# A beginning in another order, head norms with two buffers, and convolution and gate products in steps inside the attentions

## The reference, cut to what matters

```python
# first block, l = 0, 1; D = 1024
mod = silu(c) @ w_ada[l] + b_ada[l]            # 6 x 1024: shift, scale, gate for mixer and experts
h = rmsnorm(x, g_mix[l]) * (1 + sc1) + sh1
p = h @ w_in[l]        # keys, values, 8 + 8 query heads of 64, convolution 3 x 512, gates 3 x 1024
q = rope(rmsnorm(q, qg)); k = rope(rmsnorm(k, kg))       # norm over each head's 64
o_a = global attention; o_b = window attention with sinks
u = c_gate * x_in
o_c = b_gate * sum(w[j] * shifted(u, j) for j in range(3))
merged = sum over branches: sigmoid(gate) * (o @ w_branch)
x = x + gt1 * (merged @ w_out); then experts
# second block
h = rmsnorm(x, gain); p = h @ w_in
o = concat(banded(q_a, k_a, v_a) * silu(g_a), dilated(q_b, k_b, v_b) * silu(g_b))
x = x + o @ w_out
```

## Time and profile before

| | |
|---|---|
| median of 3 runs | 3480.6 us (3479.89 to 3485.04) |
| profiled execution | 3479.74 us, span 3477.7 us, mean granted TensorE clock 0.979 |
| PE busy | 3198.9 us, 92% |
| DVE, ACT busy | 1075.6 us (31%), 641.6 us (18%) |
| DMA | 551.85 MB, mean 159 GB/s |

### The profile page before, as it was taken

The page is one execution under the profiler, slowest core; times in us unless marked ns, Lnnn a source line. Parts: engine busy times, 40 slices in busy tenths (PEclk is TensorE's granted clock), DMA queues, the critical chain, the costliest instruction groups (busy, mean ns, idle before and its releaser), DMA issues. The chain is left out here.

```text
span 3477.7 us, 35357 instructions
## 1 busy us (share of the span) xinstructions
PE 3198.9 (92%) x13776; PEld 1568.4 (45%) x13776; DVE 1075.6 (31%) x1541; ACT 641.6 (18%) x1124; POOL 16.7 (0%) x35
## 2 busy tenths in 40 slices
PE   6989999999997999999988999999789889888978
PEld 3565555555553333333343654444423324343544
DVE  2566644555422010101036561011300010036241
ACT  3137500000011111111121560000111101021151
POOL 1000000000000000000000000000000000000000
PEclk8999999999998999999999999999899999999999
DMA  7020033443414878787830201223198988942200
GB/s 222 0 73 1 1 121 115 145 150 105 139 49 154 304 285 307 285 304 289 303 93 0 73 1 55 73 73 103 37 376 346 404 355 352 405 114 49 61 1 25
DMA packets 305434, 551.85 MB, mean 159 GB/s; under 512 B 62744, under 2 KB 145960, under 8 KB 305160
## 3 DMA queue, kind: packets, MB, share of 16 engines
q1 hardware_dynamic: 303376, 546.53, 44.2%
q0 software_dynamic: 1600, 3.20, 0.3%
q10 hardware_dynamic: 312, 0.05, 0.0%
HBM read 547.63 MB, written 2.10 MB: 158 GB/s over the span
## 5 line engine op out<-in xcount | busy, mean ns | idle before, releaser
L736 PE MATMUL ps<-hT,ring 128*128 128x512 f32 (+1 forms) x2576 | 969.6, 534 | 29.5 <-ACT hT L1259 27.7
L736 PEld LDWEIGHTS ps<-hT,ring 128*128 128x128 f32 x2576 | 492.6, 192 | 494.1 <-issue 464.4
L1013 PE MATMUL ps<-ring,hT 128*64 128x512 f32 x1536 | 356.9, 600 | 64.4 <-DMA ring<-in_w_e_up 35.5
L992 PE MATMUL ps<-ring,hT 128*64 128x512 f32 x1536 | 350.8, 598 | 1.5 <-ACT hT L1259 1.5
L1013 PEld LDWEIGHTS ps<-ring,hT 128*64 128x64 f32 x1536 | 100.2, 136 | 311.1 <-issue 159.3
L1906 DVE SCALAR_TENSOR_TENSOR xT<-ps,mod,xT 128x512 f32<-128x512 f32 x96 | 63.5, 662 | 498.7 <-PE ps L1099 281.1
L992 PEld LDWEIGHTS ps<-ring,hT 128*64 128x64 f32 x1536 | 101.8, 136 | 235.6 <-issue 235.1
L736 PE MATMUL ps<-obuf,ring 128*128 128x512 f32 (+1 forms) x512 | 198.5, 540 | 1.3 <-issue 1.3
L998 PE MATMUL ps<-ring,hT 128*32 128x512 f32 x1536 | 184.7, 598 | 0.0
L1591 DVE SCALAR_TENSOR_TENSOR vbuf<-ring,silc,vbuf 128x1024 f32<-128x1024 f32 x140 | 179.9, 1285 | 5.7
L1259 ACT ACTIVATE prob<-ps 128x512 f32<-128x512 f32 (+1 forms) x56 | 38.6, 688 | 673.7 <-PE ps L736 673.7
(11 more groups left out here) (223 smaller groups left out, 2471.0 us busy)
## 6 DMA issues: line engine op xcount, KB each, us to landing
ring<-in_w_e_gate SPq DMA_DIRECT2D x128, 512.0 KB, 7.2
ring<-in_w_e_up SPq DMA_DIRECT2D x128, 512.0 KB, 7.1
ring<-in_w_e_down SPq DMA_DIRECT2D x128, 512.0 KB, 6.9
ring<-in_w_e_gate SPq DMA_DIRECT2D x64, 1024.0 KB, 10.6
ring<-in_w_e_up SPq DMA_DIRECT2D x64, 1024.0 KB, 10.7
ring<-in_w_e_down SPq DMA_DIRECT2D x64, 1024.0 KB, 10.7
ring<-in_w_in SPq DMA_DIRECT2D x49, 1024.0 KB, 5.6
ring<-in_w_ada SPq DMA_DIRECT2D x48, 1024.0 KB, 6.8
```

What stands on the lines that cost most here:

```text
L736: mm = pe.matmul(ps[:, b + a:b + e], lhs[:, k, :], rhs[:, k, a:e], start=k == 0, stop=k == nk - 1)
L992: mm = pe.matmul(ps[e * CX:(e + 1) * CX, b + pair * 512:b + (pair + 1) * 512], lhs[:, k, s0:s0 + CX], expert_dst(0, slot, e)[:, k % 2, :], ...
L1013: mm = pe.matmul(ps[e * CX:(e + 1) * CX, b + h * 512:b + (h + 1) * 512], lhs[:, k, s0:s0 + CX], expert_dst(1, slot, 0)[:, e, h * 512:(h + ...
```

## The change

- **Beginning.** c and c_ctx are ACT's first loads and are turned on their own (`cond`), so silu(c) doesn't wait for the parameters. SP issues ten chunk loads before the larger part of the constants. The two first modulation groups are split along the input features instead of the output (`adf`, four chunks for each group, contiguous rows), added up in one PSUM bank and turned once for each group (`adft`). ACT squares each tile of x as soon as it is copied, DVE adds the squares, and PE sums once (`ns`). The meeting is gone.
- **Norms.** The reciprocal and the scaling are done for 512 columns first, then for the rest; the gain moves from DVE's scaling to ACT's shift (as its scale); the first product waits only for the half that it reads.
- **Head norms.** Squares alternate between `sq` and a row of `prob`, roots between `rs` and another; the sine product goes to a third row; rotations come one tile later.
- **Steps in attentions.** `conv_c` and `conv_x` of layers 0 and 1, and the last four `silg`, are taken out of the dense list. They are cut into steps (two matmuls of 512 columns, or four of 256), one behind the scores of each unit, in PSUM bank `BANK[4]`, which gets a slot of its own (`SIDE`). All value sums share `BANK[3]`. In layer 2 the transposed exponentials of the banded half stand in the unused columns of `hT`.
- **Silu.** x * sigmoid(x) becomes x * (1 + tanh(x/2)), and the factor 0.5 goes into the copy of the inverted row sums. The gates of layers 0 and 1 keep the sigmoid.

`with_modulation` is not changed.

```diff
+        roots = [rs, pr[:, 1, :]]
+        squares = [sq, pr[:, 2, :]]
+        turn_term = pr[:, 0, 0:NX]
...
+        def side_steps(l):
+            steps = []
+            if l == 2:
+                for d in range(4, 8):
+                    steps += [[("side", l, "silg", d, 0, q)] for q in range(4)]
+                    steps[-1].append(("silg", l, d))
+                return steps
+            for m in range(4):
+                for w in ("conv_c", "conv_x"):
+                    for a in range(2 - l):
+                        steps += [[("side", l, w, m, a, q)] for q in range((4, 2)[a])]
+                        steps[-1].append((w, l, m, a))
+            return steps
...
                 if s < n:
                     order.append(("S", l, s))
+                if side:
+                    order += side.pop(0)
...
-                if rots:
+                if len(rots) > 1:
                     order.append(rots.pop(0))
...
-            conv = [(f"conv_{w}", l, m) for hf in range(2) for w in "cxb" for m in (2 * hf, 2 * hf + 1)]
+            conv = [("conv_b", l, m) for m in range(4)]
...
-            first += [("v", 2, 1), ("v", 2, 2)] + [("silg", 2, d) for d in range(8)]
+            first += [("v", 2, 1), ("v", 2, 2)] + [("silg", 2, d) for d in range(4)]
...
-        FIRST = [(w, 0, n + (w == "ada")) for n in range(-1, 8) for w in ("ada", "adat") if 0 <= n + (w == "ada") < 8]
+        FIRST = [("adf", 0, 1, q) for q in range(4)] + [("ns", 0), ("adft", 0, 1)]
+        FIRST += [("adf", 0, 0, q) for q in range(4)] + [("adft", 0, 0), ("pv", 1)]
...
+                if kind == "side":
+                    w, m, a, q = j[2:]
+                    key = (w, l, m) + ((a,) if l < 2 else ())
+                    cn, slot = weights(chunk_of(j)[0])
...
+                    lo, hi, per = (0, 512, 2) if a == 0 else (512, NT, 4)
+                    for k in range(per * q, per * (q + 1)):
+                        mm = pe.matmul(ps[:, BANK[SIDE]:BANK[SIDE] + hi - lo], ring3(slot)[:, k, m % 2 * P:(m % 2 + 1) * P],
+                                       h3[:, k, lo:hi], start=k == 0, stop=k == KD - 1)
...
+                elif kind == "ns":
+                    pe.wait_ge(first_added, 1)
+                    b = begin(("norm", 0, "mix"))
+                    for a, e in halves(NT):
+                        mm = pe.matmul(ps[:, b + a:b + e], ones[:, :], h3[:, 0, a:e], start=True, stop=True)
+                    part(mm, ("norm", 0, "mix"))
...
-                        if h % 2 == 0 and n >= 2:
-                            pe.wait_ge(oT_ready.sem, n - 1)
-                    b = BANK[3 + n % 2] + h % 2 * 2 * P
+                        if h % 2 == 0 and n:
+                            pe.wait_ge(oT_ready.sem, n)
+                    b = BANK[HEAD_SUMS] + h % 2 * 2 * P
...
             sp.dma_start(tok[:, 4:6, :], ctx_in[0].rearrange("(t p) d -> p t d", p=P)).then_inc(s_x, 16)
+            for n in range(RING + 4):
+                load(n)
             sp.dma_start(con[:, C_ROT:C_HELD], consts[:, C_ROT:C_HELD]).then_inc(s_const, 16)
...
+            for d in range(KD):
+                if d % 2:
+                    A.need(xT_ready, d)
+                else:
+                    b = A.read(("xT", d))
+                    A.do(sc.copy(xT[:, d, :], ps[:, b:b + NT]))
+                    A.release(("xT", d))
+                A.do(func(h3[:, d, :], xT[:, d, :], ACT.Square), sq_ready, ("n", 0, "mix", d))
...
             def norm(ph, w):
-                key = ("norm",) + ph
-                V.need(rms_ready, key)
-                V.do(v.reciprocal(rs[:, 0:w], rs[:, 0:w]))
...
+                V.need(rms_ready, ("norm",) + ph)
+                for a, e in halves(w):
+                    V.do(v.reciprocal(rs[:, a:e], rs[:, a:e]))
+                    scaled(ph, a, e, 0, KD)
...
-                    V.do(v.tensor_tensor(sg2[:, d, :], g, ps[:, b:b + w], ALU.mult), gate_used, j)
+                    V.do(v.scalar_tensor_tensor(sg2[:, d, :], g, 1.0, ps[:, b:b + w], ALU.add, ALU.mult), gate_used, j)
```

More of the change, by code:

```diff
@@ L289, in attention_order @@
                     order.append(("T", l, s - 1, 2))
+            assert not side
             return order
@@ L720, in norm_sum @@
                 for d in range(KD):
-                    need(sq_ready, ("n",) + ph + (d,))
-                    for a, e in halves(w):
-                        mm = pe.matmul(ps[:, b + a:b + e], ones[:, :], m3[:, d, a:e], start=d == 0, stop=d == KD - 1)
-                part(mm, key)
+                    norm_piece(b, ph, m3, d, w)
+                part(norm_piece.last, key)
             seen_h = set()
@@ L1115, in _ @@
                 part(mm, ("xT", d))
-            for l in range(DEPTH):
-                pe.wait_ge(s_param[l], PARAM_DMAS[l] * 16)
-                b = begin(("pv", l))
-                rows = PROWS[l]
-                part(pe.transpose(ps[:, b:b + rows], prob[0:rows, l, 0:P], ident[0:rows, 0:rows]), ("pv", l))
-            meet()
+            run(("pv", 0))
             for j in FIRST:
@@ new lines, in _, with turned_x, add_square @@
+            V.release(("cond", 0))
+            def turned_x(d):
+                b = V.read(("xT", d))
+                V.do(v.tensor_copy(xT[:, d, :], ps[:, b:b + NT]), xT_ready, d)
+                V.release(("xT", d))
+            def add_square(d):
+                V.need(sq_ready, ("n", 0, "mix", d))
+                return v.tensor_tensor(h3[:, 0, :], h3[:, 0, :], h3[:, d, :], ALU.add)
+            turned_x(1)
+            for d in range(3, KD, 2):
+                turned_x(d)
+                V.do(add_square(d - 2))
+                V.do(add_square(d - 1))
@@ L1632, in run @@
                 w = width(l, j[2] if kind in ("qk", "hs") else "")
-                if kind == "adat":
-                    modulation(j)
+                if kind == "ns":
+                    V.need(rms_ready, ("norm", 0, "mix"))
+                    V.do(v.reciprocal(rs[:, 0:NX], rs[:, 0:NX]))
                 elif kind == "acc":
```

361 lines of the change are left out of this document (200 added, 161 removed).

## The result

| | before | after |
|---|---|---|
| median, 4 runs each | 3481.86 us (3479.89 to 3485.04) | 3382.06 us (3377.78 to 3384.78) |
| ratio, 95% interval | | 0.9711 (0.9695 to 0.9728) |
| profiled execution, span | 3479.7, 3477.7 us | 3384.8, 3382.8 us |

The change makes the kernel 2.9% faster; the forecast was 3386. The spans differ by 94.9 us. First the page of the kernel after: its span, PE's total, and the group of the steps.

The account below looks back on a forecast made before the run. PE was taken to set the end everywhere, so closed PE idleness counts in full. Terms of -27.5 - 10.8 - 6.5 + 15 - 2.6 - 21 - 2 - 23.5 - 15 = -93.9 gave 3386 us; range 3364 to 3412, some 18% outside.

Parts of the forecast that it names:

- Beginning: Start of the kernel: first product at 42 us instead of 69.64, a gain of 27.5 us (22 to 33).
- Rival 4: Beginning: the start is bound by chunks, not by the norm; first product near 52, 3396 us in all; 10%.
- The ring: Head norms: single square and root buffers make PE wait; breaking it gains 10.8, 21 and 23.5 us in layers 0, 1, 2.
- rival 2: Head norms: two buffers move the ring to DVE instead of breaking it; half of 55 us stays, 3413 us; 10%.
- Steps in layers 0 and 1: Attentions of layers 0 and 1: products moved in as steps fill PE's holes, net gains 6.5 and 2 us.
- Layer 2's steps: Layer 2's attention, first half: steps go into 16 short units, 55.7 us; net gain 15 us (10 to 18).
- Layer 0's modulation: Layer 0's dense part: eight modulation items fall among router and output products, PE waits before `rsum`; loss 15 us (8 to 19).
- Rival 1: Layer 0's dense part: the eight stray modulation items cost little, since DVE reaches them early; 3371 us; 12%.
- The table rival: Layer 2's attention: each of four tanhs needs two table loads among exponentials, some 6 us, 3392 in all; 4%.
- Rivals 3, 5 and 6: For 5: in attentions, DVE waits for each step before score reads, every unit serialises; 3530 us at 1.5 per step; 3%.
- rival 3: Attentions: a step delays DVE's or ACT's in-order queue, 0.3 to 0.5 us more in each of 96; 3424 us; 10%.
- Rival 6: Attentions: holes were closed already, counted so for layers 0 and 1; if also in layer 2, 3400 us; 5%.

## Why the prediction was right, and where its terms were off

- **Beginning, 27.5 forecast, 28.9 measured.** The transposes at 14.6 (14.24), the reciprocal from 32.5 to 36 (31.68 to 35.03), the last chunk at 39 (37.06), the first product at 42 (40.76). The chain was right in order; only the chunks came 2 us sooner than forecast, and for another reason than the forecast's. It took 3.8 us off 42.7 for the constants' new place, at 300 GB/s, and left the chunks' own pace alone. The constants' place gave 2.3; the other 3.3 go with chunks that come 2.55 us apart instead of 3.0. The constants were in time: the first head sum starts at 63.17 without a wait. Rival 4, a first product near 52, is out.
- **Head norms.** The ring was the cause, as undoing it shows: 12.1, 21.3 and 24.6 us for 10.8, 21 and 23.5. The 10.8, and the 18 and 19 behind the other two, are the idle time of the rows (9.5, 16.9 and 17.9 us) with 0.16 added for each gap. My account of which part breaks the ring was wrong in weight. I gave it to the two buffers with the later rotation; the row of its own for the sine product, taken first, brings 26.7 of the 58, and of the other two one is then enough. That DVE would need about 7.2 of 8.69 us, so that PE binds, held: no gap stands before a rotation, and rival 2 is out.
- **Layer 0's norm stage, 10.8 forecast, 13.8 measured.** Besides the 12.1 of the ring, 1.7 us are there even with the head norms undone, 1.0 of it at the first two products, a stretch that varies by more than that among kernels which don't touch it. The forecast counted the split norm in layer 1 alone, and had nothing there for the 1.5 us beyond the first product.
- **Steps in layers 0 and 1, 6.5 and 2 forecast, 5.5 and 0.7 measured.** A step costs 1.82 us, as counted with 1.84. The later rotation takes 2.9 and 1.0 at the attentions' starts, which I had costed at nothing. So the 2.44 before layer 0's second unit, the largest hole that the steps were to fill, is 2.53 in after with a slow row behind it (2.93); without the later rotation it is 1.08 and the gain 8.4 and 1.7. Convolution operations in DVE's queue took 2.2 us in layer 0 where I had 1. In layer 1 the forecast's own terms, +4 and 10 less 4.5, give -1.5 and not -2.
- **Layer 2's steps, 15 forecast, 12.1 measured.** The first half was forecast as 55.7 and took 55.84 (3203.76 to 3259.60). The rest is the half behind it, 53.1 where before had 50.0. The gaps there are nearly before's own; what is new is the stretch of slow clock, which nine of eleven kernels have. At full clock it is 15.2.
- **Layer 0's modulation, +15 forecast, +15.4 measured.** Both places are where the text had them, with gaps of 7.05 (forecast: idle until 7.4 behind the branch's end) and 5.51 (5.7), and some 5 us of slow clock where I had set 2.7 to 5.4. Rival 1, that the stray items cost little, is out by the run that deals them otherwise.
- **Silu by tanh, nothing forecast.** No load in layer 2's first half; the sigmoid there costs 5.8 us. The table rival would have been true of a sigmoid.
- **Rivals 3, 5 and 6.** The 96 steps of layers 0 to 2 cost no 0.3 us each beyond their stream, and nothing serialises; rival 3's mechanism is there in two places only, the 0.95 and 1.24 us behind convolution operations. Rival 6 is half true: of layer 1 the run with the products ahead of the attention shows 0.2 us.

The misses had both signs (1.4, 3.0, 1.8 and 1.7 too little gained by the forecast; 1.0, 0.4, 0.5, 1.3 and 2.9 too much), and so the sum of -93.9 met -94.9 more closely than its terms deserve.

Open: what decides whether the clock falls behind layer 2's last step; whether the own row is needed beside second buffers and the later rotation; whether a second bank for the value sums would bring the 1.2 us or less of layer 1 (not tried); and what of the beginning's remaining 14 us belongs to which of its parts.

## What to carry to other kernels

Where a chain of one engine's operations ends in the row that the next round's first operation overwrites, try first to give the last operation a row of its own, before doubling buffers or adding lag. Here that was 27 of 58 us, and of the other two measures one was enough for the rest, while the later rotation cost 4. Work moved into a train of groups that is already closed costs what it cost; find the holes first and put the piece right in front of the wait. And when jobs leave a list into which something else is dealt by count, the dealing has to be redone, or it ends up among jobs too short to hide it (15 us here).

## What the runs showed of the hardware

- Gaps of 5.5 and 7.1 us on PE cost some 5 us more behind them: 1.94 for a group of 1.07, and 12.4 and 12.0 for products of 10.6. That is about two fifths of the idle time itself.
- The same two gaps (1.22 and 0.81 us) were followed by a granted clock of 0.87 over 53 us in one execution (0.54 over 14 us of nearly full work) and 1.00 in another. A forecast of a few microseconds behind such gaps can't be kept.
- A switch of ACT's table costs its load of 1.28 us and nothing more that the rows show; with two loads per gate, PE lost 1.5 us per gate (5.8 by 4).
- The loads of the beginning move at 347 GB/s with the DMA engines busy for 0.98 of the time; 1120 KB set ahead of the last chunk delayed it by 2.3 us.
- Chunks of 1024 KB in pieces of 4 KB released PE 2.55 to 2.58 us apart, in pieces of 1 KB 3.01 us apart. The shape was not changed alone.
